# Moving POOL's product of z's gate with the output norm's weight in the step of a hybrid mixer and MoE kernel

## The chip, the cores and the metric

One of the cores of a Trainium2 chip runs the whole kernel. The metric is the device time of one execution in microseconds, as the median of several runs. The names of the engines are PE (matrix), PEld (PE's weight loads), DVE (vector), ACT (scalar), POOL (GpSimd) and SP (the queue that starts most DMAs).

## What is computed

The input is x, 4096 tokens of 1024 floats, with 16 learned tokens ahead. A first part mixes along the tokens, and a second part is a sparse mixture of 32 experts. The first part projects the normed tokens to 3080 columns (xb, gb, q, k, v, z and a few more), runs a convolution of width 4 over xb, q, k and v, and then has two branches:

```python
y_lru = rmsnorm(h * gelu(gb), lru_out_norm)          # branch 1; h: a linear recurrence
A = where(strict, k k^T * decay * beta, 0)           # branch 2, per head and chunk
sol = triangular_solve(I + A, [v * beta, k * beta * exp(G)])
o = rmsnorm(o, out_norm) * silu(z)
y = concat([y_lru, y_dn]) @ w_out
```

The change concerns two lines of this: `silu(z)`, which has to be multiplied with a weight, and the sums of squares that y_lru's rmsnorm needs. The triangular solve is what PE and DVE are busy with around them.

## The kernel before

The tokens are cut into 33 tiles of 128. Each engine runs its own list of instructions; the lists are written out by hand, in a function `body(s)` per engine, and `steps` (line 111) calls it for i = -2 to 35. Step i works on several tiles at once, in different stages: F (load and norm of tile i+2), P (projection, convolution, gates of tile i+1), G (the two branches of tile i), O and R (output projection and router of older tiles), S (scatter of the router's choice). The engines meet at semaphores; `need(engine, semaphore, count)` is a wait. An engine runs its list in order, so a wait holds all that stands behind it.

Within a step PE puts small matmuls of the solve between blocks of the projection of the next tile (`project`, L645, 24 matmuls a block). The solve of a 128-token tile doubles the size of the solved blocks level by level, from 2 to 7. A level goes: PE multiplies (`level_y`, L804), ACT copies the result out (L1069), PE multiplies again (`level_x`, L817), DVE puts it into X where a mask allows (L1523, a predicated copy), and DVE transposes X into `dec` for the next level (L1512, L1513). After level 6 PE transposes X itself (L934, into the bank bT), and ACT copies that into T (L1278) for level 7.

Between those links DVE does the convolutions: `conv` has for each of four taps four instructions of 128x128, the first by `tensor_scalar` (L1358 for xb, L1360 for the others), the other three by `scalar_tensor_tensor` (L1356), which reads the projected columns (`ext_q` for q) and the sum so far (`qs` for q), both in SBUF, and writes the sum. Around level 6 of the solve DVE's list is:

```python
level_x(s, 5)
conv(s, 1, qs, 2)
conv(s, 1, qs, 3, heads=range(0, 2))
level_x(s, 6)
conv(s, 1, qs, 3, heads=range(2, 4))
```

These are six L1356 between the transposes of level 5 and L1523 of level 6. The text calls them taps one to six.

POOL's list of a step, with the lines: the decay matrices (L2048, L2050, L2053, L2054), two scattered DMAs (L2061), the recurrence's input (L2066), the product zg = zs * sd (L2078), the decay of the even rows (L2001), y = h times its gate (L2085), the decay of the odd rows (L2010), the two sums over y's squares (L2091, L2093), and, after DVE's last convolution, the gated input of the next tile (L2017). `zs` is silu(z), written by ACT late in the step before (L1306); `sd` is one number per partition, a scale by which the gate is brought to the output weight's size; `zg` is read by DVE in the next step (`delta_rows`, L1542), where the normed output o is multiplied with it. ACT may overwrite zs once zg is there (semaphore `zg_ready`), DVE may read it likewise. In steps 1 and 2 POOL also copies parts of the output weight (`o_copied`, L2025); in step 2 six of these copies stand right ahead of the product.

After the last tile a second program part runs the experts, with other code; the change does not touch it.

Of the kernel before, what the change touches and what calls it, by code (L numbers as in the profile page):

```python
# [49 lines left out]
GW_SET, BA_SET, SD_SET, GSO_SET, WOG_SET = 1, 11, 13, 23, 26  # L50
Y_TOP = 11.4 * 2.0 ** 18

ALU = mybir.AluOpType
# [63 lines left out]
def need(eng, sem, value):  # L117

    if not (isinstance(value, int) and value <= 0):
        eng.wait_ge(sem, value)  # L120


def hymba_block(nc, xm, w_in, w_out, conv_w, lru_cols, w_r, w_i, mix_g, ffn_g, final_g, dn_g, dn_a,
                dn_dt, w_router, b_router, w_gate, w_up, w_down, out):
    with ExitStack() as ctx:
        def sb(name, shape, dt=F32):
            return ctx.enter_context(nc.sbuf_tensor(name, shape, dt))
# [3 lines left out]
        def sem(name):  # L131

            if name not in sems:
                sems[name] = nc.alloc_semaphore(name=name)
            return sems[name]
# [37 lines left out]
        def w_half(high, c, width, off=0, n=None):  # L173

            a = 2 * c + (width if high else 0) + off
            return slice(a, a + (n or width))
# [28 lines left out]
        sd = sb("sd", [P, 1])  # L205
# [31 lines left out]
        zs = sb("zs", [P, 4, P])  # L237
        zg = sb("zg", [P, 4, P])
# [194 lines left out]
        def cols(t):  # L433

            return t.unsqueeze(1).to_broadcast([P, 4, P])
# [27 lines left out]
        def o_room(n):  # L463

            return ht[:, 256 * (n % 4):256 * (n % 4) + 256].bitcast(F16)
# [22 lines left out]
        with nc.Block() as block:  # L488
# [1471 lines left out]
            def _(pool):  # L1960
                def high_copied(g):

                    pool.wait_ge(sem("w_low"), g + 1)
                    for k in range(KT):
                        a = nc.gpsimd.tensor_copy(w16[:, k, w_half(True, COL[GROUPS[g]], 512)], high_room(g, k))  # L1965
                    a.then_inc(sem("w_split"), 1)
# [30 lines left out]
                def even_decay(s):  # L1997

                    need(pool, sem("gates_out"), 2 * s.pP + 1)
                    need(pool, sem("a_step"), 2 * s.nG)  # L2000
                    nc.gpsimd.tensor_tensor(la[0:HALF], even[0:HALF], cl[0:HALF].unsqueeze(2).to_broadcast([HALF, 4, P]), ALU.mult  # L2001
                                            ).then_inc(sem("la_even"), 1)

                def odd_decay(s):

                    need(pool, sem("gates_out"), 2 * s.nP)
                    need(pool, sem("la_even"), s.nP)
                    need(pool, sem("y_lru"), s.nG)
                    need(pool, sem("scattered"), 32 * s.nS)
                    nc.gpsimd.tensor_tensor(la[HALF:P], odd[HALF:P], cl[HALF:P].unsqueeze(2).to_broadcast([HALF, 4, P]), ALU.mult  # L2010
                                            ).then_inc(sem("la_ready"), 1)
                    need(pool, sem("la_ready"), s.nP)

                def gated_input(s):

                    need(pool, sem("i_moved"), 32 * s.nP)
                    nc.gpsimd.tensor_tensor(gx[:], gx[:], xc[:], ALU.mult).then_inc(sem("gx_ready"), 1)  # L2017

                def o_copied(s, pieces):

                    if isinstance(s.i, int) and s.i in pieces:
                        for n in range(*pieces[s.i]):
                            k, half = divmod(n, 2)
                            pool.wait_ge(sem("o_low"), n + 1)
                            nc.gpsimd.tensor_copy(wo16[:, k, w_half(True, 512 * half, 512)], o_room(n)).then_inc(sem("o_split"), 1)  # L2025

                def body(s):
                    if s.i == -2:
                        level_masks()
                    if s.i == -1:  # L2030
                        for g in range(4):
                            high_copied(g)
                        for rest in (u_rows, h_rows):
                            pool.dma_start(rest[SEQ:SEQ + P, :], ht[:]).then_inc(sem("idx_zeroed"), 16)
                        for n in range(IDX_FILLS):
                            pool.dma_start(idx_tab.rearrange("(p n) o -> p (n o)", p=P)[:, 512 * n:512 * n + 512],
                                           fill).then_inc(sem("idx_zeroed"), 16)
                        high_copied(4)
                        even_decay(s)
                        odd_decay(s)  # L2040
                        high_copied(5)
                        gated_input(s)
                        return
                    if s.G:
                        need(pool, sem("beta_ready"), s.nG)
                        need(pool, sem("M_raw"), 2 * s.pG)
                        need(pool, sem("i_moved"), 32 * s.pP)
                        nc.gpsimd.tensor_tensor(decb[:], cols(upto16[:]), rows(nbeta[:]), ALU.mult).then_inc(sem("pool_ready"), 1)  # L2048
                        need(pool, sem("vn_full"), s.pG)
                        nc.gpsimd.tensor_copy(X[:], cols(ident[:])).then_inc(sem("pool_ready"), 1)  # L2050
                        need(pool, sem("pool_ready"), 2 * s.pG + 1)
                        need(pool, sem("dec_exp"), s.nG)
                        nc.gpsimd.tensor_tensor(decb[:], decb[:], dec[:], ALU.mult).then_inc(sem("dec2_ready"), 1)  # L2053
                        nc.gpsimd.tensor_tensor(dec[:], dec[:], cols(upto16[:]), ALU.mult).then_inc(sem("dec2_ready"), 1)  # L2054
                    if s.S:
                        if isinstance(s.i, int) and s.nS == 1:
                            pool.wait_ge(sem("idx_zeroed"), ZEROED)
                        need(pool, sem("pos_ready"), s.nS)
                        need(pool, sem("gates_ready"), s.nS)
                        for a in range(2):  # L2060
                            pool.indirect_dma_start(out=idx_tab, out_offset=bass.IndirectOffsetOnAxis(ap=posi[:, a:a + 1], axis=0),  # L2061
                                                    in_=tokg[:, a, :], in_offset=None).then_inc(sem("scattered"), 16)
                    if s.G:
                        need(pool, sem("ib_step"), 2 * s.nG)
                        need(pool, sem("gx_ready"), s.nG)
                        b = nc.gpsimd.tensor_tensor(gx[:], gx[:], hh, ALU.mult)  # L2066
                        if isinstance(s.i, int) and s.i == 0:

                            b.then_inc(sem("early_pool"), 1)
                            pool.wait_ge(sem("early_pool"), MASK_STEPS + 1)  # L2070
                            b = nc.gpsimd.memset(gx[:, :, 0:PAD], 0.0)
                        b.then_inc(sem("b_ready"), 1)
                        o_copied(s, {2: (10, 16)})
                        if isinstance(s.i, int) and s.nG == 1:
                            pool.wait_ge(sem("set_step"), SD_SET)
                        need(pool, sem("z_done"), s.nG)
                        need(pool, sem("yt_ready"), s.nO)
                        nc.gpsimd.tensor_scalar(zg[:], zs[:], sd[:], None, ALU.mult).then_inc(sem("zg_ready"), 1)  # L2078
                    if s.P:
                        even_decay(s)  # L2080
                    if s.G:
                        need(pool, sem("hl_saved"), s.nG)
                        need(pool, sem("gb_done"), s.nG)
                        need(pool, sem("yl_ready"), s.nO)
                        nc.gpsimd.tensor_tensor(yg[:], hh, gg[:], ALU.mult).then_inc(sem("y_lru"), 1)  # L2085
                    if s.P:
                        odd_decay(s)
                    o_copied(s, {1: (0, 8)})
                    if s.G:
                        need(pool, sem("y_sq"), s.nG)  # L2090
                        nc.gpsimd.tensor_tensor(aa[:, 0:2, :], aa[:, 0:2, :], aa[:, 2:4, :], ALU.add).then_inc(sem("y_sum"), 1)  # L2091
                        need(pool, sem("y_sum"), 2 * s.pG + 1)
                        nc.gpsimd.tensor_tensor(aa[:, 0, :], aa[:, 0, :], aa[:, 1, :], ALU.add).then_inc(sem("y_sum"), 1)  # L2093
                    o_copied(s, {1: (8, 10)})
                    if s.P:

                        need(pool, sem("conv"), 16 * s.nP)
                        gated_input(s)
# [391 lines left out]
```

## Time and profile before

| | |
|---|---|
| median of three runs | 3183.18 us (3181.97 to 3184.43) |
| the profiled execution | 3177.59 us, of which the profile's span is 3176.0 us |
| busy, share of the span | PE 92%, PEld 68%, DVE 81%, ACT 62%, POOL 30% |
| instructions of POOL | 993, with 937.5 us |
| mean granted clock of PE | 0.966 of full speed |

The span is one execution on the one core. Busy shares are means over the whole span; the pipeline over the tiles and the experts have different ones. Times in rows are microseconds from the span's start unless marked ns. A row of the order of time gives start, duration, engine, line, operation, tile written and tiles read, shapes and count, and in brackets how long the engine had been idle and who released it.

### The profile page before, as it was taken

The page shows a single profiled execution, that of the slowest core. Times are in us where ns is not written, and L with a number is a line of the kernel's source. Part 1 is how long each engine was busy: PE and PEld are TensorE (multiplying, and loading weights), DVE is VectorE, ACT ScalarE, POOL GpSimd, SP SyncE. Part 2 cuts the span into 40 slices and gives each one's busy share as a digit, 9 for nine tenths or more (in the row PEclk, how much of TensorE's full clock was granted, in tenths as well). Part 3 has the DMA queues.
Part 4 walks back from the last instruction along what each step waited for, and adds up shares of the span by engine and source line. Part 5 has one row for each costly group of instructions (what it writes and reads, how often), then busy time and mean ns, then how long its engine had stood idle before and what let it go on. Part 6 is the DMA issues. An engine that isn't in the chain of part 4 may idle for free. (4 is left out here: it accounts for less than half of the span.)

```text
span 3176.0 us, 81781 instructions
## 1 busy us (share of the span) xinstructions
PE 2911.7 (92%) x28516; PEld 2159.1 (68%) x28517; DVE 2569.2 (81%) x7201; ACT 1970.1 (62%) x4385; POOL 937.5 (30%) x993
## 2 busy tenths in 40 slices
PE   4778999999999999999999999995899999999960
PEld 4776878888878888887888788773444555554530
DVE  6888778888888888888888888885887888888844
ACT  6555666565656566666656666652676777776746
POOL 4422222122223212222322222231343444444420
PEclk9899999999999999999999999997999999999985
DMA  6111233333332322223232322315587777777749
GB/s 232 62 50 28 88 94 94 86 88 84 88 94 75 94 85 84 88 88 95 75 92 84 87 84 88 92 61 209 163 264 215 232 215 194 197 213 224 225 99 396
DMA packets 224451, 413.33 MB, mean 130 GB/s; under 512 B 121104, under 2 KB 121104, under 8 KB 211856
## 3 DMA queue, kind: packets, MB, share of 16 engines
q1 hardware_dynamic: 187232, 303.01, 29.7%
q0 software_dynamic: 29216, 89.30, 12.3%
q10 hardware_dynamic: 7696, 16.86, 1.4%
q8 instruction: 201, 3.29, 0.4%
q14 instruction: 106, 0.87, 0.1%
HBM read 280.06 MB, written 96.01 MB: 118 GB/s over the span
## 5 line engine op out<-in xcount | busy, mean ns | idle before, releaser
L645 PE MATMUL pj<-uT,W 128*128 128x128 f16 x15744 | 977.5, 220 | 12.5 <-POOL W L1965 12.5
L645 PEld LDWEIGHTS pj<-uT,W 128*128 128x128 f16 x15744 | 927.2, 98 | 44.8 <-issue 31.1
L2346 DVE SCALAR_TENSOR_TENSOR W<-W,ecol 128x512 f16<-128x512 f16 x664 | 447.4, 746 | 108.8 <-ACT W L2290 107.5
L2290 ACT ACTIVATE W<-W,ecol 128x512 f16 x664 | 415.9, 708 | 84.0 <-issue 77.2
L2254 PE MATMUL bA<-W,uT 128*128 128x512 f16 x1992 | 446.7, 381 | 5.6 <-issue 4.3
L2254 PEld LDWEIGHTS bA<-W,uT 128*128 128x128 f16 x1992 | 193.3, 98 | 229.0 <-issue 10.0
L2238 PE MATMUL pj<-W,qs 128*128 x664 | 303.0, 599 | 3.0 <-issue 2.1
L2017 POOL TENSOR_TENSOR gx<-gx,xc 128x512 f32<-128x512 f32 x33 | 42.5, 1287 | 672.0 <-DVE vs L1356 672.0
L1039 ACT ACTIVATE ht<-ht 128x512 f32<-128x512 f32 x256 | 160.3, 637 | 101.4 <-DMA ht<-w_up 93.0
L1069 ACT ACTIVATE qh<-bA 128x256 f32<-128x256 f32 x198 | 77.8, 393 | 230.8 <-PE bA L804 229.7
L2238 PEld LDWEIGHTS pj<-W,qs 128*128 128x128 f32 x664 | 121.1, 192 | 125.3 <-issue 124.8
L708 PE MATMUL bO<-W,yl 128*128 128x512 f16 x768 | 186.1, 382 | 5.0 <-DVE yl L1588 5.0
L1356 DVE SCALAR_TENSOR_TENSOR qs<-ext_q,cvw,qs 128x128 f32<-128x128 f32 x384 | 184.3, 533 | 1.1
L662 PE MATMUL pj<-W,uT 128*128 128x512 f16 x768 | 181.3, 379 | 0.0
L708 PE MATMUL bO<-W,yt 128*128 128x512 f16 x768 | 180.4, 381 | 0.0
L2001 POOL TENSOR_TENSOR lath<-even,cl 64x512 f32<-64x512 f32 x33 | 35.6, 1078 | 429.4 <-ACT even L1079 429.4
L804 PE MATMUL bA<-dec,Mt 128*128 128x128 f32 x792 | 138.1, 297 | 17.2 <-DVE dec L1513 14.5
L2214 POOL DMA_INDIRECT h_rows<-lath,sid x42 | 72.8, 1733 | 251.4 <-issue 127.0
L2214 POOL DMA_INDIRECT h_rows<-aahh,sid x41 | 68.9, 1680 | 201.3 <-issue 99.0
L804 PEld LDWEIGHTS bA<-dec,Mt 128*128 128x128 f32 x792 | 105.5, 192 | 32.5 <-DVE dec L1513 27.2
L817 PE MATMUL bB<-X,qh 128*128 128x128 f32 x660 | 114.6, 297 | 8.4 <-ACT qh L1069 8.4
L662 PEld LDWEIGHTS pj<-W,uT 128*128 128x128 f16 x768 | 71.6, 98 | 68.4
(501 smaller groups left out, 6091.8 us busy)
## 6 DMA issues: line engine op xcount, KB each, us to landing
ht<-w_gate SPq DMA_DIRECT2D x128, 256.0 KB, 3.5
ht<-w_up SPq DMA_DIRECT2D x128, 256.0 KB, 3.3
W<-w_gate SPq DMA_DIRECT2D x32, 1024.0 KB
W<-w_up SPq DMA_DIRECT2D x32, 1024.0 KB
W<-w_down SPq DMA_DIRECT2D x32, 1024.0 KB
x_in<-xm SPq DMA_DIRECT2D x33, 512.0 KB, 4.4
ht<-xm SPq DMA_DIRECT2D x32, 512.0 KB, 4.2
h_rows<-ht SPq DMA_DIRECT2D x32, 512.0 KB
```

Of the source, the lines that this page charges most:

```text
L645: mm = pe.matmul(pj[g % 2][:, j, :], w16[:, k, w_half(w_high, COL[GROUPS[g]], 512, j * P, P)], (ul if low_u else uh)[:, k, :], start=(k == ...
L662: mm = pe.matmul(flat(pj[1]), u[:, k, :], w16[:, k, w_half(w_high, c, 512)], start=(k == 0 and n_pass == 0), stop=(k == KT - 1 and n_pass ...
L708: mm = pe.matmul(bOf[:, 512 * half:512 * half + 512], y, wo16[:, j, w_half(w_high, 512 * half, 512)], start=(j == 0 and not w_high), stop= ...
L804: mm = pe.matmul(bA[:, q, :], Mt[:, 2 + q, :], crossed(T, b, P * q, HALF // b), start=True, stop=True)
L817: mm = pe.matmul(bB[:, q, :], Y[:, q, :], crossed(X, b, P * q, HALF // b), start=True, stop=True)
L1039: nc.scalar.activation(ht[:, 512 * (c % 2):512 * (c % 2) + 512], ht[:, 512 * (c % 2):512 * (c % 2) + 512], ACT.Square, accum_out=sqc[:, n, ...
L1356: a = nc.vector.scalar_tensor_tensor(out=to, in0=src, scalar=w, in1=to, op0=ALU.mult, op1=ALU.add)
L2214: pool.indirect_dma_start(out=h_rows, out_offset=bass.IndirectOffsetOnAxis(ap=sid[par][:], axis=0), in_=yo[par], in_offset=None, compute_o ...
L2238: mm = pe.matmul(flat(pj[half]), hm2[:, j, :], w[:, j, 512 * half:512 * half + 512], start=(j == 0), stop=(j == 1))
L2254: mm = pe.matmul(flat(bA), x[:, k, :], wx[par][:, part, k, :], start=(k == 0 and part == 0 and x is uh), stop=(k == KT - 1 and x is ul))
L2290: nc.scalar.activation(part_of(wx[par][:, 0], k), raw[:, k], ACT.Copy, scale=ecol[par][:, k:k + 1]).then_inc(sem("wx_high"), 1)
L2346: a = nc.vector.scalar_tensor_tensor(out=part_of(wx[par][:, 1], k), in0=raw[:, k], scalar=ecol[par][:, k:k + 1], in1=part_of(wx[par][:, 0] ...
```

## The change

POOL's product is taken from its place behind the recurrence's input and put behind the second sum over y's squares, with the three waits that stood before it (the one on `sd` in the first step, that zs is there, and that DVE has read the old zg). Nothing else changes, no engine but POOL has another list, and what is computed is the same.

```diff
@@ -2071,11 +2071,6 @@
                             b = nc.gpsimd.memset(gx[:, :, 0:PAD], 0.0)
                         b.then_inc(sem("b_ready"), 1)
                         o_copied(s, {2: (10, 16)})
-                        if isinstance(s.i, int) and s.nG == 1:
-                            pool.wait_ge(sem("set_step"), SD_SET)
-                        need(pool, sem("z_done"), s.nG)
-                        need(pool, sem("yt_ready"), s.nO)
-                        nc.gpsimd.tensor_scalar(zg[:], zs[:], sd[:], None, ALU.mult).then_inc(sem("zg_ready"), 1)
                     if s.P:
                         even_decay(s)
                     if s.G:
@@ -2091,6 +2086,11 @@
                         nc.gpsimd.tensor_tensor(aa[:, 0:2, :], aa[:, 0:2, :], aa[:, 2:4, :], ALU.add).then_inc(sem("y_sum"), 1)
                         need(pool, sem("y_sum"), 2 * s.pG + 1)
                         nc.gpsimd.tensor_tensor(aa[:, 0, :], aa[:, 0, :], aa[:, 1, :], ALU.add).then_inc(sem("y_sum"), 1)
+                        if isinstance(s.i, int) and s.nG == 1:
+                            pool.wait_ge(sem("set_step"), SD_SET)
+                        need(pool, sem("z_done"), s.nG)
+                        need(pool, sem("yt_ready"), s.nO)
+                        nc.gpsimd.tensor_scalar(zg[:], zs[:], sd[:], None, ALU.mult).then_inc(sem("zg_ready"), 1)
                     o_copied(s, {1: (8, 10)})
                     if s.P:
```

On POOL, in a step in the middle of the pipeline, this order stands before:

```order
L2061 DMA idx_tab<-tokg,posi 131072x2 x2
L2066 TENSOR_TENSOR gx<-gx,aahh 128x512
L2078 TENSOR_SCALAR zg<-zs,sd 128x512
L2001 TENSOR_TENSOR lath<-even,cl 64x512
L2085 TENSOR_TENSOR yg<-aahh,gg 128x512
L2010 TENSOR_TENSOR lath<-decb,cl 64x512
L2091 TENSOR_TENSOR aahh<-aahh 128x256
L2093 TENSOR_TENSOR aahh<-aahh 128x128
L2017 TENSOR_TENSOR gx<-gx,xc 128x512
```

and this one now (the lines of the changed kernel: 2080 for 2085, 2086 and 2088 for the sums, 2093 for the product):

```order
L2061 DMA idx_tab<-tokg,posi 131072x2 x2
L2066 TENSOR_TENSOR gx<-gx,aahh 128x512
L2001 TENSOR_TENSOR lath<-even,cl 64x512
L2080 TENSOR_TENSOR yg<-aahh,gg 128x512
L2010 TENSOR_TENSOR lath<-decb,cl 64x512
L2086 TENSOR_TENSOR aahh<-aahh 128x256
L2088 TENSOR_TENSOR aahh<-aahh 128x128
L2093 TENSOR_SCALAR zg<-zs,sd 128x512
L2017 TENSOR_TENSOR gx<-gx,xc 128x512
```

The product has moved past five instructions and stands last before the wait for DVE's last convolution.

## Rows read from the trace of the kernel before

**Rows 1.** Busy us by engine (instructions), TensorE clock, DMA share, GB/s, in the pipeline's stretch

```profile
135.00:2170.00 2035.00, 1984.46 (x24034) 1650.14 (x24032) 1713.23 (x5494) 1220.52 (x2972) 502.12 (x464) 0.99 0.29 84
```

**Rows 2.** Waits of PE's weight loads, 430 to 2110: total us, times, longest

```profile
PEld bA L804 <- DVE dec L1513: 9.6, 54, 0.2
```

**Rows 3.** POOL in order of time: start, us, line, idle before it and its releaser

```profile
1212.29 1.28 POOL L2066 TENSOR_TENSOR gx<-gx,aahh 128x512 f32<-128x512 f32 x1 [1.83 <-ACT aahh L1225]
1213.55 1.56 POOL L2078 TENSOR_SCALAR zg<-zs,sd 128x512 f32<-128x512 f32 x1
1228.90 1.07 POOL L2001 TENSOR_TENSOR lath<-even,cl 64x512 f32<-64x512 f32 x1 [13.79 <-ACT even L1079]
...
1234.50 0.46 POOL L2093 TENSOR_TENSOR aahh<-aahh 128x128 f32<-128x128 f32 x1
1256.28 1.28 POOL L2017 TENSOR_TENSOR gx<-gx,xc 128x512 f32<-128x512 f32 x1 [21.32 <-DVE vs L1356]
...
1275.44 1.57 POOL L2078 TENSOR_SCALAR zg<-zs,sd 128x512 f32<-128x512 f32 x1
```

**Rows 4.** DVE beside the product; L1358 over the whole trace (ns min/median/max)

```profile
1214.21 0.68 DVE L1824 TENSOR_TENSOR kd<-bT,ekd 128x512 f32<-128x512 f32 x1
...
L1358 DVE TENSOR_SCALAR xc<-ext_xb,cvw,lcol x128: 335/342/386, 136.9 to 2083.0; 128x128 f32<-128x128 f32 x128
```

**Rows 5.** DVE's fifth and sixth tap, and L1523

```profile
1234.60 0.50 DVE L1356 SCALAR_TENSOR_TENSOR qs<-ext_q,cvw,qs 128x128 f32<-128x128 f32 x1
...
1235.03 0.34 DVE L1356 SCALAR_TENSOR_TENSOR qs<-ext_q,cvw,qs 128x128 f32<-128x128 f32 x1
1235.29 0.43 DVE L1523 COPY_PREDICATED X<-lvl,bB 128x256 f32<-128x256 uint8 x1
```

**Rows 6.** PE's weight load for the transposes, same step

```profile
1235.92 0.42 PEld L934 LDWEIGHTS bT<-ident,X 128*128 128x128 f32 x4
```

**Rows 7.** Step i=2: the product, taps 1 and 2, taps 1 to 3 (ns), taps 3 and 4

```profile
290.74 1.59 POOL L2078 TENSOR_SCALAR zg<-zs,sd 128x512 f32<-128x512 f32 x1
...
290.20 1.39 DVE L1356 SCALAR_TENSOR_TENSOR qs<-ext_q,cvw,qs 128x128 f32<-128x128 f32 x2
...
L1356 DVE SCALAR_TENSOR_TENSOR qs<-ext_q,cvw,qs x3: 340/691/774, 290.2 to 291.5; 128x128 f32<-128x128 f32 x3
...
291.51 0.60 DVE L1356 SCALAR_TENSOR_TENSOR qs<-ext_q,cvw,qs 128x128 f32<-128x128 f32 x2
```

**Rows 8.** Step i=2: level 6 on DVE, and the load that waited for it

```profile
297.96 0.43 DVE L1523 COPY_PREDICATED X<-lvl,bB 128x256 f32<-128x256 uint8 x1
...
298.44 0.42 PEld L934 LDWEIGHTS bT<-ident,X 128*128 128x128 f32 x4 [0.61 <-DVE X L1523]
```

**Rows 9.** DVE's fourth L1542 beside POOL's additions

```profile
1205.57 1.38 DVE L1542 SCALAR_TENSOR_TENSOR yt<-ot,ors,zg 128x128 f32<-128x128 f32 x1
...
1205.53 1.27 POOL L2053 TENSOR_TENSOR decb<-decb,dec 128x512 f32<-128x512 f32 x1 [2.42 <-ACT dec L1194]
1206.77 1.21 POOL L2054 TENSOR_TENSOR dec<-dec,upto 128x512 f32<-128x512 f32 x1
```

**Rows 10.** Later on DVE: the wait for PE, and the product's reader

```profile
1247.29 0.69 DVE L1874 TENSOR_TENSOR ot<-ot,bC 128x512 f32<-128x512 f32 x1 [0.91 <-PE bC L959]
...
1266.68 2.18 DVE L1542 SCALAR_TENSOR_TENSOR yt<-ot,ors,zg 128x128 f32<-128x128 f32 x4
```

**Rows 11.** L1523 and load L934: step 3, step 4 (L1523 alone), step 31

```profile
359.58 0.43 DVE L1523 COPY_PREDICATED X<-lvl,bB 128x256 f32<-128x256 uint8 x1
...
360.21 0.42 PEld L934 LDWEIGHTS bT<-ident,X 128*128 128x128 f32 x4
...
426.63 0.44 DVE L1523 COPY_PREDICATED X<-lvl,bB 128x256 f32<-128x256 uint8 x1 [4.28 <-PE bB L817]
...
2102.66 0.43 DVE L1523 COPY_PREDICATED X<-lvl,bB 128x256 f32<-128x256 uint8 x1
...
2103.30 0.42 PEld L934 LDWEIGHTS bT<-ident,X 128*128 128x128 f32 x4
```

## The prediction

> **What bounds the kernel.** I read the busy time by stage first. Of the 3176 us, the pipeline over the 33 tiles takes the stretch 135 to 2170, and there PE is busy 1984 of 2035 us at a granted clock of 0.99 [rows 1]. The changed line runs in this stretch only. So the question is whether PE gets a new gap in a tile's step (about 61.9 us: POOL's product starts at 1213.55 and again at 1275.44 [rows 3]). Next the waits of PE's weight loads: in steady steps the only wait of size on another engine is line 804 on DVE's transpose L1513, 54 times and 9.6 us, under 0.2 us each [rows 2]. Both kinds follow a matmul of PE's own, so they travel with PE; they are not slack that could swallow a new delay. A delay that makes PE wait even 0.3 us is paid in every step.
>
> **What the change removes.** POOL's product zg (L2078) takes 1.56 us, between L2066 and 13.8 us of idle [rows 3]. Nobody waits for it there: its reader, DVE's L1542, comes at 1266.68, in the next step [rows 10], and ACT overwrites its source zs only with the tile after, behind z's projection. POOL's next instruction waits for ACT. Did it cost DVE anything there? L1824 ran beside it in 0.68 us, as in all steps, and one of its source tensors lies in PSUM; behind it come four L1358 of one tensor each, and of all 128 in the trace the longest took 0.386 us against a median of 0.342 [rows 4]. So at most 0.04 us of DVE a step comes back, 32 x 0.04 = 1.4 us if PE had waited for all of it. It does not: a DVE that comes earlier here waits for PE's next level. I cost the removal at **0**; what covers it is POOL's idle time and DVE's one-tensor work.
>
> **What it adds.** The product now stands behind L2093, which runs 1234.50 to 1234.96 [rows 3]. Its three semaphores are long set, so it should follow back to back, as it followed L2066 (0.02 us before that row's end [rows 3]): 1234.94 to 1236.5. POOL's next, L2017, comes at 1256.28 [rows 3], so POOL itself, y's sums for the norm and the next step lose nothing. What stands beside the product is new: DVE's L1356, a convolution tap whose two tensors (ext_q and qs) both lie in SBUF.
>
> The trace shows what such taps suffer. Undisturbed one takes 0.34 us (the one at 1235.03 [rows 5]). Under POOL's additions it stands until the POOL instruction ends: of the six at this place the fifth, at 1234.60, takes 0.50 us, ending 0.14 us after L2093 [rows 5, 3]. The same at L1542, issued at 1205.57: 1.38 us, ending 0.15 us after L2053's 1205.53 + 1.27 [rows 9].
>
> For the product against a tap there is one instance, and it is almost this case. In step i=2 six copies of POOL stand ahead of the product, which therefore runs late, at 290.74, amid four L1356 [rows 7]. The first tap (from 290.20) was waiting for the copy and took 0.69 us, the median of the three in that row, so it ended at 290.89, 0.15 us into the product. The second, the longest of the three, took 0.774 us: it began 0.08 us after the product and ended 1.39 us after 290.20, at 291.59. That is 0.43 us over 0.34. The third and fourth, at 291.51, took 0.60 us for both, undisturbed, though the product ran until 292.33. So the product keeps a tap out for about its first 0.7 us, not for all its 1.59 us.
>
> In the steady step the phases will be the same to 0.01 us: product at 1234.94, fifth tap ending 1235.10 (0.16 us into it), sixth issued at 1235.03 (0.09 us after its start). I take **0.43 us** for the sixth tap. L1523, the solve's level 6, follows it: it starts at 1235.29 and ends at 1235.72 [rows 5]; now 1236.15.
>
> PE's transposes L934 need it. Their weight load starts at 1235.92, right as the L645 block lets it [rows 6]. In step i=2 L934 did wait for L1523, which ended at 297.96 + 0.43 = 298.39, and loaded at 298.44 [rows 8]: the hand-over takes 0.05 us. So the load comes at 1236.15 + 0.05 = 1236.20, and PE stands 1236.20 - 1235.92 = **0.28 us** (of the 0.43 us, 0.20 - 0.05 = 0.15 us is slack).
>
> **Which steps pay.** The distance from L1523's end to the load is 0.20 us in step 3 (360.01 to 360.21) and 0.21 in step 31 (2103.09 to 2103.30), and 0.19 to 0.22 in all others between, but for step 4, where ACT reads two experts' sums and L1523 waits 4.28 us for a late PE, so that DVE has caught up [rows 11]. That is 28 steps: 3 and 5 to 31. Steps 0, 1 and 32 have more slack than 0.43 us, and no such tap right behind L2093. Step 2 is mixed: the product no longer stops the tap at 290.82, but L2001 moves up into its place, an addition that runs 1.07 us when undisturbed [rows 3] and stops the tap longer (1.07 + 0.15 us past 290.74 + 0.15 against 291.59, some 0.5 us later); PE, waiting at level 6, loses that and regains most at L934, where it had waited 0.61 us [rows 8]; net I put +0.2 us.
>
> **Is it given back?** After L934 the other engines go by PE again: DVE, 0.43 us late against PE's 0.28, idles 0.91 us for PE at L1874 [rows 10], which swallows the 0.15 us. The next step starts in the old phase. The period is 61.9 + 0.28.
>
> **Sum.** 28 x 0.28 = 7.8, plus 0.2 for step 2, minus 0: **+8.0 us**. The profiled execution took 3177.59 us (its span is 3176.0), so it would take 3185.6; the median of the three runs shown, 3183.18 us, lies 5.6 above the profiled one, and I add the same 8.0: **3191.2 us**. About 0.2% (6.4 us) is what a measurement of this kernel can tell from no change.
>
> The unknown price is the tap's delay. Low end 0 (rows 4: one-tensor neighbours of the product were not delayed), high end 1.28 us, the product held to its end as L2053 was (1234.94 + 1.57 + 0.14 = 1236.65, against 1235.37). I take 0.43, the same pair of instructions in the same phase. Within that mechanism 0.33 to 0.55 us seems possible, a stall of 0.18 to 0.40 us, 5.2 to 11.4 us in all.
>
> **Rivals.**
> (a) No stall, 3183.2 us. The sixth tap gets in ahead of the product, or the product starts late enough for it. It decides at 0.15 us of delay: below that L934's load is not late. For it: taps already queued do get in between two POOL instructions (L1542 ended although L2054 followed back to back at 1206.77 [rows 9]). Against: the sixth tap is issued after the product, and in step 2 the same did not get in.
> (b) The product holds DVE to its end: 1.28 - 0.15 = 1.13 us a step, 28 x 1.13 = 31.6 us, 3214.8 us. For it: every addition of POOL does [rows 5, 9]. Against: taps three and four of rows 7. The Trainium skill, "SBUF — State Buffer", section "Who interferes with whom", states this rule: a VectorE instruction with two SBUF inputs contends with a GpSimd instruction that reads SBUF, and the one that comes second is blocked for the whole instruction of the other. By it the time would be this rival's. The additions here agree (0.50 and 1.38 us); the product of step 2, two taps of 0.30 us spacing inside it, does not.
> (c) Between the two: the product is granted later and stops the sixth tap for 0.6 to 0.9 us; 28 x 0.6, about 3200 us.
> (d) Faster: the freed place helps DVE more than rows 4 say and the sixth tap is spared. It needs PE to be waiting for DVE's L1523 of the level before; at 0.04 us a step this is 1.4 us, 3182.
>
> **How the numbers follow.** Forecast 0.72, (a) 0.15, (b) 0.06, (c) 0.04, (d) 0.03. The range holds the forecast's own band and most of (a): 3183 to 3196. Slower by over 0.2%: four fifths of the forecast's 0.72 (its band reaches below 6.4 us), with (b) and (c): 0.68. Faster by over 0.2% needs a gain no row shows: 0.03. The rest, 0.29, is within 0.2%.
>
> **What would show it.** In the changed profile: the product right behind the second sum; the sixth tap at 0.77 us instead of 0.34; a new wait of PE's load L934 on DVE's L1523, some 28 times, 0.28 us each, in all near 8 us; steps of 62.2 us; L1874's wait down by 0.15 us. If the tap stays at 0.34 us, (a) holds; if it takes 1.6 us, (b). If L934 waits as said and the time does not grow, the step "is it given back" was wrong.

## The result, and the profile after

The changed kernel takes 3187.53 us (median of 20 runs, 3183.56 to 3192.91) against 3181.07 us before (20 runs of the same study). The ratio is **1.0019**, with a 95% interval of 1.0012 to 1.0026: 3.8 to 8.3 us slower, 6.0 in the middle. The forecast was +8.0 us. On total time this is at the edge of what can be told from no change; the steps tell more.

POOL in a step of the pipeline's middle (order of time, profile after):

```profile
1236.21 1.07 POOL L2001 TENSOR_TENSOR lath<-even,cl 64x512 f32<-64x512 f32 x1 [15.35 <-ACT even L1079]
...
1241.80 0.46 POOL L2088 TENSOR_TENSOR aahh<-aahh 128x128 f32<-128x128 f32 x1
1242.23 1.61 POOL L2093 TENSOR_SCALAR zg<-zs,sd 128x512 f32<-128x512 f32 x1
1263.86 1.27 POOL L2017 TENSOR_TENSOR gx<-gx,xc 128x512 f32<-128x512 f32 x1 [20.02 <-DVE vs L1356]
```

The product follows the second sum back to back, 0.03 us ahead of that row's end, and ends 20 us before POOL is wanted again; L2001's idle time ahead has grown by the product's length, from 13.79 us [rows 3] to 15.35. On DVE, beside it, the fifth tap, the sixth, and level 6:

```profile
1241.90 0.50 DVE L1356 SCALAR_TENSOR_TENSOR qs<-ext_q,cvw,qs 128x128 f32<-128x128 f32 x1
...
1242.32 0.77 DVE L1356 SCALAR_TENSOR_TENSOR qs<-ext_q,cvw,qs 128x128 f32<-128x128 f32 x1
1243.02 0.43 DVE L1523 COPY_PREDICATED X<-lvl,bB 128x256 f32<-128x256 uint8 x1
1243.35 0.34 DVE L1356 SCALAR_TENSOR_TENSOR qs<-ext_q,cvw,qs 128x128 f32<-128x128 f32 x1
```

The fifth tap is as before [rows 5]. The sixth takes 0.77 us instead of 0.34: 0.43 us, to the hundredth what the tap of step i=2 had lost [rows 7]. The tap behind L1523, still beside the product, is undisturbed. PE's load for the transposes (before: [rows 6]), and DVE's later wait for PE (before: [rows 10]):

```profile
1243.50 0.42 PEld L934 LDWEIGHTS bT<-ident,X 128*128 128x128 f32 x4 [0.24 <-DVE X L1523]
```

```profile
1254.87 0.69 DVE L1874 TENSOR_TENSOR ot<-ot,bC 128x512 f32<-128x512 f32 x1 [0.77 <-PE bC L959]
```

The load now starts 0.05 us after L1523's end (1243.02 + 0.43). The 0.24 us in brackets is idle time after the last load's end; counted from where it could start it is 0.28 us, as loads overlap by 0.04. DVE's wait for PE shrinks from 0.91 to 0.77 us. From 430 to 2120 us the new wait is there 27 times, once in each of steps 5 to 31, and L804's [rows 2] is as it was:

```profile
PEld bA L804 <- DVE dec L1513: 9.7, 54, 0.2
PEld bT L934 <- DVE X L1523: 6.5, 27, 0.2
```

**Where the difference of the two profiled executions lies.** They took 3177.59 and 3188.51 us, with spans of 3176.0 and 3186.4, 10.4 us apart. I cut both spans at the loads of L934. To step 0's load (160.6 against 163.6 us): +3.0. Steps 1 and 2: +1.0. Steps 3 to 31 (298.44 to 2103.30, against 302.48 to 2114.47): +7.1. The rest: -0.7. The first 3.0 us arise ahead of the product's first place (135.6 us in the profile before), where both orders are the same: POOL's first L2053 starts at 128.6 and at 131.9 us. So the change itself accounts for about 7 of the 10.4.

### The profile page after: what moved, and what is told of

Read it like the earlier page. It is cut to its first block and busy times, and to the rows that moved or that the text cites. A ratio compares the mean times of both kernels' runs of the same rounds, so it can differ in the third digit from the quotient of the medians.

```text
span 3186.4 us, 81781 instructions
## 1 busy us (share of the span) xinstructions
PE 2922.2 (92%) x28516; PEld 2165.1 (68%) x28517; DVE 2581.5 (81%) x7201; ACT 1969.6 (62%) x4385; POOL 940.4 (30%) x993
## 5 line engine op out<-in xcount | busy, mean ns | idle before, releaser
L1039 ACT ACTIVATE ht<-ht 128x512 f32<-128x512 f32 x256 | 160.3, 636 | 100.7 <-DMA ht<-w_up 92.2
L1069 ACT ACTIVATE qh<-bA 128x256 f32<-128x256 f32 x198 | 77.5, 391 | 230.3 <-PE bA L804 229.4
L1356 DVE SCALAR_TENSOR_TENSOR qs<-ext_q,cvw,qs 128x128 f32<-128x128 f32 x384 | 196.8, 565 | 1.1
L2001 POOL TENSOR_TENSOR lath<-even,cl 64x512 f32<-64x512 f32 x33 | 35.3, 1070 | 477.4 <-ACT even L1079 477.4
L804 PE MATMUL bA<-dec,Mt 128*128 128x128 f32 x792 | 137.6, 297 | 17.7 <-DVE dec L1513 14.8
L804 PEld LDWEIGHTS bA<-dec,Mt 128*128 128x128 f32 x792 | 105.1, 192 | 33.0 <-DVE dec L1513 27.5
L817 PE MATMUL bB<-X,qh 128*128 128x128 f32 x660 | 114.6, 297 | 8.1 <-ACT qh L1069 8.1
```

Of the source, the lines that this page charges most:

```text
L804: mm = pe.matmul(bA[:, q, :], Mt[:, 2 + q, :], crossed(T, b, P * q, HALF // b), start=True, stop=True)
L817: mm = pe.matmul(bB[:, q, :], Y[:, q, :], crossed(X, b, P * q, HALF // b), start=True, stop=True)
L1039: nc.scalar.activation(ht[:, 512 * (c % 2):512 * (c % 2) + 512], ht[:, 512 * (c % 2):512 * (c % 2) + 512], ACT.Square, accum_out=sqc[:, n, ...
L1356: a = nc.vector.scalar_tensor_tensor(out=to, in0=src, scalar=w, in1=to, op0=ALU.mult, op1=ALU.add)
```

## The experiments

The most exact reading of each run is the stretch from step 5's load of L934 to step 31's, 26 steps of the one profiled execution. "Last tap" is the duration of the last tap ahead of level 6 in those steps. The last column is the ratio of all runs, with its 95% interval (11 or 12 runs of each kernel, but 20 of the change, 4 of e3, 5 of e10 and 6 of e11).

| kernel | last tap, us | steps 5 to 31, us | one step | ratio to before |
|---|---|---|---|---|
| before | 0.34 | 1610.36 | 61.94 | |
| the change | 0.77 | 1617.15 | 62.20 | 1.0019 (1.0012 to 1.0026) |
| e12, the change again | 0.77 | 1617.79 | 62.22 | 1.0029 (1.0018 to 1.0040) |
| e1, behind level 6 | 0.34 | 1610.31 | 61.94 | 1.0001 (0.9990 to 1.0012) |
| e2, tap behind level 6 | 0.50 (the fifth) | 1610.23 | 61.93 | 1.0011 (1.0001 to 1.0020) |
| e3, tensor_tensor | 1.12 | 1626.56 | 62.56 | 1.0065 (1.0048 to 1.0081) |
| e5, two halves | 0.56 | 1612.17 | 62.01 | 1.0020 (1.0007 to 1.0032) |
| e6, 8 columns, old place | 0.34 | 1610.35 | 61.94 | 1.0026 (1.0015 to 1.0037) |
| e7, 8 columns, new place | 0.35 | 1610.26 | 61.93 | 1.0028 (1.0017 to 1.0039) |
| e8, other order, old place | 0.34 | 1607.27 | 61.82 | 0.9994 (0.9984 to 1.0005) |
| e9, other order, new place | 0.77 | 1607.19 | 61.82 | 0.9991 (0.9979 to 1.0003) |
| e10, second order, old place | 0.34 | 1598.53 | 61.48 | 0.9955 (0.9941 to 0.9970) |
| e11, second order, new place | 0.77 | 1598.56 | 61.48 | 0.9952 (0.9935 to 0.9968) |

(A mean step is about 0.03 us over most of its steps, 61.90 us before, since in all but e10 and e11 three of the 26 are 0.2 to 0.4 us longer.)

### e1: the product behind level 6

```diff
                         need(pool, sem("yt_ready"), s.nO)
+                        need(pool, sem("X_new"), 6 * s.pG + 5)
                         nc.gpsimd.tensor_scalar(zg[:], zs[:], sd[:], None, ALU.mult).then_inc(sem("zg_ready"), 1)
```

> The changed kernel with one more wait: POOL's product waits until DVE's L1523 of level 6 is done, so it starts about 0.8 us later, beside the convolution taps behind L1523. My theory (only the sixth tap, which stands ahead of L1523, matters): the sixth tap back to 0.34 us, no wait of PE's load L934 on L1523, steps of 61.9 us, the time of the kernel before (ratio 1.000, within 0.001). The first tap behind L1523 takes 0.77 us instead, and costs nothing. Rival (any DVE delay behind the solve's last levels is paid, or POOL's later end is): steps stay at 62.2 us, ratio about 1.002.

```profile
1242.48 1.74 POOL L2094 TENSOR_SCALAR zg<-zs,sd 128x512 f32<-128x512 f32 x1 [0.96 <-DVE X L1523]
```

```profile
1241.59 0.34 DVE L1356 SCALAR_TENSOR_TENSOR qs<-ext_q,cvw,qs 128x128 f32<-128x128 f32 x1
1241.85 0.43 DVE L1523 COPY_PREDICATED X<-lvl,bB 128x256 f32<-128x256 uint8 x1
1242.18 0.60 DVE L1356 SCALAR_TENSOR_TENSOR qs<-ext_q,cvw,qs 128x128 f32<-128x128 f32 x2
1242.82 0.55 DVE L1366 COPY ext_q<-ext_q 128x12 f32<-128x12 f32 x1
1243.28 1.09 DVE L1360 TENSOR_SCALAR ks<-ext_k,cvw 128x128 f32<-128x128 f32 x4
```

The POOL row, then DVE's. The product now starts 0.2 us after L1523's end, 0.96 us behind the second sum instead of back to back, and runs 0.13 us longer than in the changed kernel; the sixth tap is back to 0.34 us, the wait of L934 is gone, and the steady stretch is that of the kernel before to 0.05 us. DVE still loses time, 0.38 us at L1366 and 0.21 at the four L1360, but behind L1523, and it costs nothing. No tap was held, where I had expected 0.77 us for the first behind L1523: the semaphore came late, and the second of the two taps had started 0.04 us ahead of the product. It ran in 0.34 us, 0.30 us of that beside the product. The rival, that any delay of DVE or of POOL's end is paid, falls.

### e2: the sixth tap behind level 6

```diff
-                    conv(s, 1, qs, 3, heads=range(0, 2))
+                    conv(s, 1, qs, 3, heads=range(0, 1))
                     level_x(s, 6)
-                    conv(s, 1, qs, 3, heads=range(2, 4))
+                    conv(s, 1, qs, 3, heads=range(1, 4))
```

> The changed kernel with DVE's sixth tap moved behind L1523 of level 6 (conv heads 0 to 0 ahead of it, 1 to 3 behind). The product stays where the change puts it. My theory: DVE still loses about 0.43 us to the product, but behind L1523; the load L934 waits for nothing, L1523 ends about 0.26 us earlier than in the kernel before, steps of 61.9 us, ratio to the kernel before 1.000. It is not faster than before, since L934 had not waited there. Rival (the stall comes from the product's place itself, not from the tap): 62.2 us a step, ratio 1.002.

```profile
1238.38 1.61 POOL L2093 TENSOR_SCALAR zg<-zs,sd 128x512 f32<-128x512 f32 x1
```

```profile
1238.47 0.43 DVE L1523 COPY_PREDICATED X<-lvl,bB 128x256 f32<-128x256 uint8 x1
1238.80 0.70 DVE L1356 SCALAR_TENSOR_TENSOR qs<-ext_q,cvw,qs 128x128 f32<-128x128 f32 x2
```

The product stays where the change put it. L1523 starts 0.09 us after it and runs its 0.43 us: of its sources X's new part lies in PSUM, and the product does not stop it. It covers the time in which a tap would be held, so the first two of the three taps behind take 0.70 us instead of 0.60; DVE loses 0.10 there, not the 0.43 I had expected. The stretch is 1610.23 us. So it is the order on DVE that decides. The ratio of all runs, 1.0011, lies above my 1.000 and its interval leaves out 1.000 by a hair; the steady steps do not contain this difference (see e12).

### e3: the product as a tensor_tensor

```diff
-nc.gpsimd.tensor_scalar(zg[:], zs[:], sd[:], None, ALU.mult)
+nc.gpsimd.tensor_tensor(zg[:], zs[:], sd[:].unsqueeze(2).to_broadcast([P, 4, P]), ALU.mult)
```

> The changed kernel with the product as a tensor_tensor with sd spread over the row, instead of a tensor_scalar; same place. If what counts is the kind of POOL's instruction (its additions stop a tap until they end, the tensor_scalar only for its first 0.7 us), the product runs about 1.1 to 1.3 us, the sixth tap takes about 1.4 us instead of 0.77, the load L934 waits 0.9 us instead of 0.28, steps of 62.8 us: 28 x 0.9 = 25 us over the kernel before, ratio 1.008. If a tap is held alike by both kinds, the sixth tap stays near 0.77 us and the ratio near 1.002.

```profile
1251.04 1.09 POOL L2093 TENSOR_TENSOR zg<-zs,sd 128x512 f32<-128x512 f32 x1
```

```profile
1251.16 1.12 DVE L1356 SCALAR_TENSOR_TENSOR qs<-ext_q,cvw,qs 128x128 f32<-128x128 f32 x1
1252.21 0.43 DVE L1523 COPY_PREDICATED X<-lvl,bB 128x256 f32<-128x256 uint8 x1
```

```profile
1252.69 0.42 PEld L934 LDWEIGHTS bT<-ident,X 128*128 128x128 f32 x4 [0.58 <-DVE X L1523]
```

The instruction is a third shorter and costs more than twice as much. The tap stands until POOL's instruction ends (1252.13) and ends 0.15 us after it. The delay is 0.78 us and the wait 0.63, under the 0.9 I had expected. With the 1.28 us of other additions it would have been 0.82 us by the same reckoning; the 1.4 us I gave the tap was too much even then. The stretch grows by 16.2 us, 0.62 us a step, and the ratio is 1.0065. This is the hold to the end of rival (b), for the other kind of instruction.

### e5: the product in two halves

```diff
-nc.gpsimd.tensor_scalar(zg[:], zs[:], sd[:], None, ALU.mult).then_inc(sem("zg_ready"), 1)
+nc.gpsimd.tensor_scalar(zg[:, 0:2, :], zs[:, 0:2, :], sd[:], None, ALU.mult)
+nc.gpsimd.tensor_scalar(zg[:, 2:4, :], zs[:, 2:4, :], sd[:], None, ALU.mult).then_inc(sem("zg_ready"), 1)
```

> The changed kernel with the product cut in two instructions of 128x256, one behind the other, same place. If the time for which the product keeps a tap out goes with its length, the first half keeps the sixth tap out for about 0.2 us less than before: a delay of 0.15 to 0.22 us instead of 0.43, a wait of L934 of 0 to 0.07 us instead of 0.28, ratio to the kernel before 1.000 to 1.0006. If it is a fixed opening of the instruction, the sixth tap stays at 0.77 us, the wait at 0.28 us and the ratio at 1.002.

```profile
1237.86 0.56 DVE L1356 SCALAR_TENSOR_TENSOR qs<-ext_q,cvw,qs 128x128 f32<-128x128 f32 x1
1238.35 0.43 DVE L1523 COPY_PREDICATED X<-lvl,bB 128x256 f32<-128x256 uint8 x1
```

```profile
1238.83 0.42 PEld L934 LDWEIGHTS bT<-ident,X 128*128 128x128 f32 x4
```

Half the columns, half the delay: 0.22 us against 0.43. The load starts 0.05 us after L1523 and 0.07 us late, and a step of the steady stretch is 0.07 us longer. The ratio of all runs came out at 1.0020, over the 1.0000 to 1.0006 that I had given; the stretch accounts for 1.8 of these 6.4 us. Where the rest comes from was not shown (see e12).

### e6 and e7: only 8 columns, at either place

```diff
-nc.gpsimd.tensor_scalar(zg[:], zs[:], sd[:], None, ALU.mult).then_inc(sem("zg_ready"), 1)
+nc.gpsimd.tensor_scalar(zg[:, :, 0:2], zs[:, :, 0:2], sd[:], None, ALU.mult).then_inc(sem("zg_ready"), 1)
```

> The kernel before with the product, at its old place, cut to 8 of its 512 columns (the other 504 columns of zg keep old values, so the gate of branch 2 is left out there). My theory (the product costs nothing at the old place): steps of 61.9 us and the time of the kernel before, ratio 1.000 within the interval. Rival (the old place cost DVE or POOL something, so that taking it away was worth a gain that the new place ate): steps below 61.9 us by 0.04 us or more.

> The changed kernel with the product, at its new place, cut to 8 of its 512 columns (the other 504 columns of zg keep old values). If the time for which the product keeps the sixth tap out goes with its length (0.43 us at 512 columns, 0.22 at 256), almost nothing is left: the tap takes 0.34 to 0.40 us, the load L934 waits for nothing, steps of 61.9 us, ratio 1.000. If the opening has a fixed part, the tap keeps 0.1 us or more of it; below 0.15 us that still costs PE nothing.

The other 504 columns of zg keep old values in both. In e7:

```profile
1239.63 0.35 POOL L2093 TENSOR_SCALAR zg<-zs,sd 128x8 f32<-128x8 f32 x1
```

```profile
1239.72 0.35 DVE L1356 SCALAR_TENSOR_TENSOR qs<-ext_q,cvw,qs 128x128 f32<-128x128 f32 x1
```

e6 takes the product practically away at the old place, and the stretch stays at 1610.35 us: there it cost nothing, and the change had nothing to gain. e7 has the instruction at the new place without its length: the tap loses 0.01 us, the stretch is 1610.26. So there is hardly a fixed part. The ratios to the kernel before, 1.0026 and 1.0028, are not 1.000 as expected. They are alike, so the new place of these 8 columns costs nothing that can be told. The excess over the kernel before lies outside the 26 steps: in the two profiles what follows step 31's load takes 1079.7 and 1083.5 us instead of 1072.7. With old values in zg the router may pick other experts; that this is the reason was not shown, since kernels that compute zg in full take up to 1079.3 us there.

### e8 and e9: another order of DVE and PE

```diff
-                    conv(s, 1, qs, 1)
                     if s.O and s.G:
                         low_lru(s)
                     level_x(s, 5)
-                    conv(s, 1, qs, 2)
-                    conv(s, 1, qs, 3, heads=range(0, 2))
+                    conv(s, 1, qs, 1)
                     level_x(s, 6)
-                    conv(s, 1, qs, 3, heads=range(2, 4))
+                    conv(s, 1, qs, 2)
+                    conv(s, 1, qs, 3)
...
-                    project(s, 2, 1)
+                    project_some(s, 2, 1, 0, 20)
                     level_x(s, 3)
+                    project_some(s, 2, 1, 20, 24)
...
-                    project(s, 3, 1)
+                    project_some(s, 3, 1, 0, 20)
                     level_x(s, 5)
+                    project_some(s, 3, 1, 20, 24)
```

(`project_some` issues the matmuls from one number to another of a block.)

> The kernel before, product at its old place, in another order of DVE and PE. DVE: low_lru and level 5 ahead of the tap row qs 1, and the tap rows qs 2 and 3 behind level 6. PE: the last 4 of 24 matmuls of the blocks ahead of level_x(3) and level_x(5) moved behind them, so that PE has 0.22 us more to do while DVE turns X for the next level. My reading of PE's two waits for L1513 (0.17 us each a step, latency of DVE's chain behind L817): both vanish, L934 does not wait, steps of 61.9 - 0.34 = 61.56 us, 28 x 0.34 = 9.5 us less than before, ratio 0.997. Rival (DVE is the bound between level 3 and 6, and the waits only move, or level 7 waits for the convolutions pushed back): 61.7 to 62.0 us a step, ratio 0.999 to 1.001.

> The same other order of DVE and PE with the product at its new place. In this order four taps of DVE stand ahead of L1523 of level 6, and the product comes behind the second sum, near PE's L817. If, as I hold, the product costs only where a two-tensor instruction ahead of L1523 meets its opening, then the cost here is 0 to 0.28 us a step by where the taps fall; I expect the four taps to be done before the product starts, so 0.00 to 0.05 us a step over the reordered kernel with the product at its old place. Rival (the new place costs its 0.28 us in any order): 0.28 us a step, 7.8 us, more than that kernel.

PE's two waits for L1513 are gone, but two others stand in their place. The waits of e8's weight loads (500 to 2100; L963 and L1541 are the L948 and L1526 of the kernel before, L830 and L1084 its L817 and L1069):

```profile
PEld bB L963 <- DVE dec L1541: 8.4, 26, 0.3
PEld bB L830 <- ACT qh L1084: 6.2, 26, 0.2
```

The first is level 7, whose copies now stand behind a DVE that has been given more to do; the second is a block of PE made too short for ACT's copy, which stands behind the gates' eight activations there. A step falls by 0.12 us instead of 0.34, and the ratio cannot be told from 1. That is the rival I had named. e9, with the product at its new place, has the same stretch to 0.08 us: in this order the new place is free. It is not free for the reason that I had expected, four taps done before the product starts. The fourth meets it, in every steady step:

```profile
1232.11 1.61 POOL L2107 TENSOR_SCALAR zg<-zs,sd 128x512 f32<-128x512 f32 x1
```

```profile
1232.21 0.78 DVE L1371 SCALAR_TENSOR_TENSOR qs<-ext_q,cvw,qs 128x128 f32<-128x128 f32 x1
...
1233.27 0.45 DVE L1538 COPY_PREDICATED X<-lvl,bB 128x256 f32<-128x256 uint8 x1 [0.28 <-PE bB L830]
```

The 0.43 us are lost, but level 6 (here L1538) waits for PE behind the tap, and it ends 0.56 us before the load of the transposes (1234.28), as in e8.

### e10 and e11: the second order

The edit against e8 and e9:

```diff
-                    project_some(s, 3, 1, 0, 20)
+                    project(s, 3, 1)
                     level_x(s, 5)
-                    project_some(s, 3, 1, 20, 24)
                     project(s, 3, 2)
                     late_part(s, 0)
+                    project_some(s, 3, 3, 0, 4)
                     level_y(s, 6)
-                    project(s, 3, 3)
+                    project_some(s, 3, 3, 4, 24)
...
-                    conv(s, 2, ks, 0, 1, 2, 3)
+                    conv(s, 2, ks, 0, 1, 2)
                     level_x(s, 7)
+                    conv(s, 2, ks, 3)
```

> e8 mended at the two places where its profile shows new waits, product at its old place. PE: the blocks ahead of level_x(5) whole again (there PE had waited for ACT's copy of Y), and 4 matmuls of the block behind level_y(6) moved ahead of it instead. DVE: level 7's copies ahead of the last tap row of ks. If those two waits were all that ate the gain, steps of 61.56 us, 0.34 less than before, ratio 0.997. Rival (another wait comes in their place): 61.7 to 61.9 us, ratio 0.999 to 1.000.

> The same with the product at its new place. e9 against e8 showed the new place free when no two-tensor tap stands between the second sum and L1523; here the same: the step of e10 within 0.03 us, the ratio of e10.

Both waits vanish from the list and none comes in their place. A step takes 61.48 us, 0.45 less than before, and the ratio is 0.9955 (0.9941 to 0.9970; 5 runs): 3166.0 us against 3179.0 before in the same study. I had expected 0.34 us a step. The other 0.1 us is in the same two waits, which I had read too small. The profile before gives 0.17 to 0.18 us for each, and that is idle time after the end of the load ahead. Undisturbed, such loads overlap by 0.04 us: in e10 the two start 0.06 us after the start of the load ahead, where they had started 0.28 after it. So each wait was worth 0.22 us, both 0.44. In e11 the product is at its new place, and still holds a tap out:

```profile
1229.42 1.61 POOL L2110 TENSOR_SCALAR zg<-zs,sd 128x512 f32<-128x512 f32 x1
```

```profile
1229.52 0.77 DVE L1373 SCALAR_TENSOR_TENSOR qs<-ext_q,cvw,qs 128x128 f32<-128x128 f32 x1
...
1230.35 0.44 DVE L1540 COPY_PREDICATED X<-lvl,bB 128x256 f32<-128x256 uint8 x1
```

```profile
1231.37 0.42 PEld L951 LDWEIGHTS bT<-ident,X 128*128 128x128 f32 x4
```

The same 0.43 us are lost, ahead of level 6 too, and cost nothing (1598.56 against 1598.53 us): level 6 (here L1540) ends 0.58 us before the load (here L951), where the old order had 0.20. Both beat the kernel before and the changed one; between them no difference can be measured.

### e12: the change again

> The changed kernel as it is, beside the two others on one chip, to separate what a step pays from what the rest of a run brings with it. Theory: steps of 62.17 us again (0.26 above before), the sixth tap at 0.77 us in every steady step, and a ratio of 1.002; the opening, the first five steps and the experts' part vary from run to run with the clock by more than what the change costs.

The steady stretch is 1617.79 us, with most steps at 62.19 where I had expected 62.17, and the ratio 1.0029, where I had expected 1.002, inside its interval. Outside the stretch runs wander by more than the change costs: step 0's load comes between 159.5 and 165.1 us in the thirteen profiles, in no relation to the edits, and what follows step 31's load takes 1067.7 to 1079.3 us in the eleven that compute zg in full. One source is PE's granted clock. Ahead of step 0's load it was 0.94 in e2 (159.5 us, PE busy for 100.7) and 0.90 in e7 (165.1 us, PE busy for 108.3, with the same number of matmuls). Step 2 in the kernel before and in e1 (busy us by engine, clock, DMA share, GB/s):

```profile
232.60:298.40 65.80, 53.82 (x687) 47.05 (x684) 55.63 (x145) 35.60 (x78) 25.06 (x24) 0.95 0.11 26
```

```profile
235.10:303.90 68.80, 56.37 (x685) 49.76 (x683) 56.47 (x147) 35.88 (x78) 25.27 (x25) 0.90 0.11 24
```

The clock is the mean over stretches at full speed (2.4 GHz) and at half of it (1.2 GHz); in this step PE is busy some 54 of 66 us, against nearly all of a steady one. At 0.95 the step took 65.8 us, at 0.90 it took 68.8. In steps 5 to 31 PE was busy 1609 of 1610 us in the kernel before and 1614 of 1617 in the changed one, and the clock was 1.00 in both. e2's step 2 ran at 0.90 too and took 69.0 us. e5's did not (0.95, 65.8 us); there 5.8 us of excess lie behind step 31's load (1078.5 us against 1072.7, at 0.92 in both). So the clock in step 2 fits the one and not the other, and why e2 and e5 miss in the whole time and not in the steps stays open.

## Why the prediction was right

Point by point, as it had them.

**What bounds the kernel** held: PE has no slack in a steady step, and a wait of 0.28 us made the step 0.26 us longer in the one profile and 0.29 in the other (6.79 and 7.43 us over 26 steps).

**What the change removes: 0.** e6 shows it, to 0.01 us over 26 steps. (The bound on DVE's part was added up wrongly: 32 x 0.04 is 1.3, not 1.4. Nothing hangs on it.)

**What it adds.** The tap's delay was forecast from one instance in step i=2, at 0.43 us; measured 0.43. Slack 0.15 us, stall 0.28: measured 0.28. The slack is confirmed from four sides, since the wait is always the delay less 0.15 us: 0.01 gives none (e7), 0.22 gives 0.07 (e5), 0.43 gives 0.28, 0.78 gives 0.63 (e3).

**Which steps pay.** The 28 named. Steps 3 to 31 grew by 7.1 us against 7.8 forecast in the one profile; e12's stretch, at 0.29 us a step, would give 8.0. The two bracket the forecast. The delay of L934 itself is the same in both, 7.3 and 7.2 us over the 26 steps, or 0.28 a step; the difference lies in small waits of other loads, which fell by 0.5 us in the one and grew by 0.2 in the other. **Step 2** was mis-sized: 65.8 to 66.4 us, +0.6, where I had put +0.2. I had PE regain at L934 most of what it lost at level 6. But here too the product met the sixth tap, which took 0.77 us, so nothing was regained: L934's idle time grew from 0.61 to 0.71 us. I had left that out of the step's sum. In e7, where no tap is held, the step takes 65.8 us. Even the 0.6 us depends on the clock: e12's step 2, at 0.90, took 68.8 us like e1's, and L934 waited for nothing in either.

**Is it given back?** No. DVE's wait at L1874 fell by 0.14 us, where 0.15 was forecast.

**The sum** was +8.0; measured +6.0, with an interval of 3.8 to 8.3, and 9 us (5.7 to 12.7) in e12. Both intervals hold 8.0. The time itself came out at 3187.5 us against 3191.2: 2.1 of the 3.7 us are the base (median 3183.18 of three runs, 3181.07 of twenty), the rest is 6.5 us between the medians instead of 8.0. I had given 0.68 to "slower by over 0.2%"; 1.0019 lies just under that line and e12's 1.0029 over it, so the runs do not settle on which side the change falls.

**The rivals.** (a), the tap slips in: no step of the steady stretch shows it. (b), the product holds DVE to its end: it did not. The tap was delayed by 0.43 us, where a hold to the end would have delayed it by 1.33 (1243.84 + 0.15 against 1242.66). Such a hold is the rule of the Trainium skill ("SBUF — State Buffer", section "Who interferes with whom"). For POOL's tensor_tensor the traces agree with it (e3, the sums), for its tensor_scalar they do not. Had the product been written as a tensor_tensor, the price would have been 0.62 us a step (e3). (c) and (d) did not occur.

## What to carry to other kernels

A free instruction is free at its place: before moving one to an engine's idle time, list what the engine that it can hold up (here DVE) does there, and what that engine does next that somebody waits for. The delay alone says little; a delay of 0.43 us cost 0.28 us ahead of level 6 with 0.15 us of slack, and nothing where level 6 had over 0.5 us to spare (e9, e11) or stood ahead of the held tap (e2, with 0.10 us left of the delay). And look for an odd step: here a disturbed one (i=2) already contained the collision, with the price to the hundredth.

## What the runs showed of the hardware

POOL's tensor_scalar keeps DVE's two-tensor instruction out only in its first part, and that part goes with the columns: 0.01, 0.22 and 0.43 us of delay for 8, 256 and 512. POOL's tensor_tensor keeps it out to 0.15 us past its end. For the same 512 columns the tensor_scalar ran 1.56 to 1.74 us and the tensor_tensor 1.09: the longer instruction delayed the tap by 0.43 us, the shorter by 0.78.

In e1 the product met DVE instructions of one tensor, which had not collided in rows 4: L1366 took 0.55 us instead of 0.17, and of the four L1360 the longest 0.63 us, against 0.28 to 0.29 in the changed kernel:

```profile
L1360 DVE TENSOR_SCALAR ks<-ext_k,cvw x4: 274/388/630, 1243.3 to 1243.9; 128x128 f32<-128x128 f32 x4
```

```profile
L1360 DVE TENSOR_SCALAR ks<-ext_k,cvw x4: 280/282/286, 1244.1 to 1244.7; 128x128 f32<-128x128 f32 x4
```

(ns min/median/max; e1, then the changed kernel). In the steady steps of e1 the first two of the four, issued 0.8 and 1.0 us into the product, took 0.27 us each, undisturbed. The third and fourth, issued 1.2 and 1.4 us in, took 0.63 and 0.50 and ended 0.1 us behind the product's end. A tap issued 1.4 us into the product (1243.61 in the changed kernel) took its 0.34 us. So for a one-tensor DVE instruction with a single constant the last part of the product counts too, which a tap passes freely. The product was itself 0.13 us longer there; which of the two held the other first was not tried. What tells L1358 (two constants, unhurt) from L1360 (one) was not tried.
